# Softmax shares applied by TensorE: a product with a diagonal matrix in place of scaling and turning

## The reference, cut to what matters

```python
p = softmax(where(mask, q @ k.T * scale, -1e30))     # over the branch's keys
o = g[..., 0:1] * (p_c @ v_c) + g[..., 1:2] * (p_s @ v_s) + g[..., 2:3] * (p_w @ v_w)
```

## Time and profile before

| what | value |
|---|---|
| time, median of 3 | 2161.82 us (2155.26 to 2162.44) |
| profiled execution | 2147.99 us |
| its span, first to last instruction | 2146.1 us |
| TensorE busy | 1712.8 us, 80% |
| VectorE busy | 558.3 us, 26% |
| ScalarE busy | 391.6 us, 18% |
| GpSimd busy | 63.7 us, 3% |
| mean granted TensorE clock | 0.928 |

### The profile page before, as it was taken

The page is one execution under the profiler, slowest core; times in us unless marked ns, Lnnn a source line. Parts: engine busy times, 40 slices in busy tenths (PEclk is TensorE's granted clock), DMA queues, the critical chain, the costliest instruction groups (busy, mean ns, idle before and its releaser), DMA issues.

```text
span 2146.1 us, 21293 instructions
## 1 busy us (share of the span) xinstructions
PE 1712.8 (80%) x7510; PEld 803.9 (37%) x7510; DVE 558.3 (26%) x1722; ACT 391.6 (18%) x937; POOL 63.7 (3%) x115
## 2 busy tenths in 40 slices
PE   5998888898888777777369988888978878778772
PEld 2863333344333323332138633434443323223321
DVE  4761334435100000000247603344350000000002
ACT  3111333212111111011031123332121110110110
POOL 0000000000000000000100000000000000000001
PEclk9999999999899999999679999999989989989896
DMA  5421000341799999999343211003427999999993
GB/s 142 97 79 40 26 34 20 113 204 76 312 427 427 429 429 427 429 428 428 146 132 69 79 40 40 20 20 152 172 108 311 428 428 427 429 427 428 429 427 146
DMA packets 119166, 505.73 MB, mean 236 GB/s; under 512 B 37936, under 2 KB 74800, under 8 KB 94512
## 3 DMA queue, kind: packets, MB, share of 16 engines
q1 hardware_dynamic: 107280, 461.75, 53.6%
q0 software_dynamic: 7200, 26.22, 3.2%
q10 hardware_dynamic: 4608, 16.78, 1.9%
HBM read 481.65 MB, written 23.07 MB: 235 GB/s over the span
## 4 chain that ended last, share of the span: by engine, by line
PE 51%; DMA 31%; ACT 5%; DVE 4%; SPq 3%; issue 3%; POOL 1%; POOLq 0%; ACTq 0%; DVEq 0%
DMA arena<-in_expert_up 16%; PE bank L951 14%; DMA arena<-in_expert_gate 12%; PE bank L649 11%; PE bank L670 10%; PE bank L864 5%; SPq L517 3%; PE bank L799 2%; PE bank L831 2%; ACT arena L1128 2%; DMA arena<-in_expert_down 2%; DVE nbias L1550 1%; PE bank L821 1%; PE bank L702 1%; ACT arena L1142 1%
## 5 line engine op out<-in xcount | busy, mean ns | idle before, releaser
L951 PE MATMUL bank<-arena 128*64 128x512 f32 x2688 | 739.6, 637 | 144.5 <-DMA arena<-in_expert_up 86.7
L951 PEld LDWEIGHTS bank<-arena 128*64 128x64 f32 x2688 | 253.8, 146 | 480.8 <-issue 480.8
L670 PE MATMUL bank<-hT,arena 128*128 128x512 f32 x512 | 272.4, 630 | 16.4 <-ACT arena L1107 15.0
L1718 DVE TENSOR_TENSOR arena<-arena,bank 128x512 f32<-128x512 f32 x32 | 22.0, 688 | 909.8 <-PE bank L951 909.8
L951 PE MATMUL bank<-spare_slot,arena 128*64 128x512 f32 x384 | 188.0, 647 | 48.6 <-DMA arena<-in_expert_up 24.7
L1550 DVE TENSOR_REDUCE nbias<-bank 128x1 f32<-128x31 f32 (+4 forms) x192 | 61.6, 383 | 248.8 <-PE bank L802 125.5
L864 PE MATMUL bank<-arena,hT 128*128 128x512 f32 x256 | 113.4, 596 | 4.2 <-DVE hT L1593 4.2
L951 PEld LDWEIGHTS bank<-spare_slot,arena 128*64 128x64 f32 x384 | 55.3, 149 | 163.5 <-issue 163.5
L670 PEld LDWEIGHTS bank<-hT,arena 128*128 128x128 f32 x512 | 85.0, 196 | 79.8 <-issue 50.5
L1128 ACT ACTIVATE arena<-bank,nbias 128x31 f32<-128x31 f32 (+4 forms) x192 | 83.3, 446 | 171.1 <-DVE nbias L1550 139.9
L649 PE MATMUL bank<-arena,hT 128*128 128x256 f32 (+1 forms) x512 | 114.2, 384 | 0.0
(11 more groups left out here) (327 smaller groups left out, 1409.9 us busy)
## 6 DMA issues: line engine op xcount, KB each, us to landing
arena<-in_expert_gate SPq DMA_DIRECT2D x56, 2048.0 KB, 28.1
arena<-in_expert_up SPq DMA_DIRECT2D x56, 2048.0 KB, 30.5
arena<-in_expert_down SPq DMA_DIRECT2D x56, 2048.0 KB, 29.5
arena<-in_w_in SPq DMA_DIRECT2D x26, 1024.0 KB, 5.8
spare_slot<-in_expert_gate SPq DMA_DIRECT2D x8, 2048.0 KB, 26.5
spare_slot<-in_expert_up SPq DMA_DIRECT2D x8, 2048.0 KB, 29.9
y_rows<-arena ACTq DMA_DIRECT2D x32, 512.0 KB, 10.2
spare_slot<-in_expert_down SPq DMA_DIRECT2D x8, 2048.0 KB, 26.9
```

Of the source, the lines that this page charges most:

```text
L670: r = pe.matmul(bank[:, FB, :], lhs, rhs, start=(k == 0), stop=last)
L951: r = pe.matmul(dst[CAP * e:CAP * e + CAP, :], moving[:, k, CAP * e:CAP * e + CAP], slot_of(first + e)[:, k, cols], start=(k == 0), stop=( ...
L1718: TT(hid, silu, bank[:, 3, :], ALU.mult).then_inc(act_ready, 1)
```

## The change

Line 1565's four in-place scalings of `prob` go. In their place VectorE writes one matrix per head, `share`: the identity times the head's shares, in one instruction of 128x512 elements. TensorE then multiplies each block of `prob` (unscaled) by that diagonal matrix, by an ordinary float32 product, where it had turned the scaled block with the identity. The result in PSUM is the same: keys on partitions, each query's column times its share. `share` has two buffers by the parity of n, in a part of the arena that nothing else uses during attention. TensorE waits once for a unit's `share` instead of four times for the scalings.

```diff
+        share = view(126, 2, 4, P)
...
                     c = c0 + kt
                     if c >= 2:
                         pe.wait_ge(evac_act if c % 2 == 0 else evac_dve, c // 2)
+                    if kt == 0:
+                        pe.wait_ge(p_ready, n + 1)
                     for i in range(4):
-                        if kt == 0:
-                            pe.wait_ge(p_ready, 4 * n + i + 1)
-                        r = pe.transpose(bank[0:w, 4 + c % 2, P * i:P * i + P],
-                                         prob[:, n % 2, i, P * kt:P * kt + w], ident[:, :])
+                        r = pe.matmul(bank[0:w, 4 + c % 2, P * i:P * i + P],
+                                         prob[:, n % 2, i, P * kt:P * kt + w], share[:, n % 2, i, :], start=True, stop=True)
                     r.then_inc(tr_done, 1)
...
-                    nk = NCMP if br == CMPB else P * (qt + 1)
                     s = rscale[:, n % 2, :]
...
-                    for i in range(4):
-                        pr = prob[:, n % 2, i, 0:nk]
-                        TS(pr, pr, s[:, i:i + 1], None, ALU.mult).then_inc(p_ready, 1)
+                    TT(share[:, n % 2], mid(ident[:, :], 4), bc(s, P), ALU.mult).then_inc(p_ready, 1)
```

## The result

| | before | after |
|---|---|---|
| time, median (5 runs each) | 2158.34 us (2155.26 to 2162.44) | 2176.11 us (2172.49 to 2181.65) |
| ratio | | 1.0088, 95% interval 1.007 to 1.0106 |
| span of the profiled execution | 2146.1 us | 2170.6 us |
| attention stretch, layer 0 / layer 1 | 196.91 / 196.94 us | 208.02 / 208.01 us |

The change makes the kernel slower by 0.88%. That ratio is not the one of the two medians, which lie 17.8 us or 0.82% apart. The stretches of the last row begin with the first score product and end with the first product of the merge. A second set of runs of the same two kernels gave 1.0126 (1.0095 to 1.0157), medians 2157.19 and 2179.95 us: 22.8 us.

What follows compares the result with a forecast made beforehand. It took attention to be bound by TensorE's turns where no gap hides them: 5.2 + 3.9 + 1.3 + 0 - 0.1 = 10.3 us per layer, 20.5 us for two, giving 2182 us; range 2170 to 2204.

Steps and rivals of the forecast that it cites:

- The second record: On TensorE, a float32 product takes two records where a turn takes one, adding 0.43 us per group of four.
- (a): Attention units in query tiles 0 to 3 where turns set the pace: 12 groups paid in full, 5.2 us per layer.
- (b): Turns of key tiles 2 and 3 in other units, between value products: 9 groups in full, 3.9 us per layer.
- (c): Units with small gaps ahead of the first value product, absorbing part of the added time: 1.3 us per layer remains.
- (d): First two key tiles of other units, 19 groups ahead of gaps of 0.69 us or more: costs nothing.
- the last unit: Attention unit without following scores to hide behind; saved scalings pay for eight more passes, gaining 0.06 us.
- Where it lands: Unit-by-unit placement of 48 groups per layer in attention, costing 10.3 us per layer, 20.5 us for two.
- The clock, 0 in the sum: TensorE clock falls in attention cost 3.3 us per layer; counted as 0, with plus or minus 6.6 in the range.
- no cover: Rival: every added TensorE pass in attention shows, +41 us, 2203 us; chance 0.12 for between forecast and this rival.
- hidden: Rival: copies, not turns, set the attention inner loop's pace; 7.5 us left, 2169 us; chance 0.11.
- faster: Rival: VectorE's queue bounds attention, so saved scalings give 18.6 us back, 2143 us; chance 0.04.
- four times: Rival: on TensorE a product costs four turns' passes, a group growing by 1.3 us, 2244 us; chance 0.03.

Runs made afterwards that it cites:

- run 6: Kernel before, turns of key tiles 0 and 1 issued twice in the 14 units per layer with gaps of 0.69 us or more; ratio to before 1.0008.
- run 2: Kernel before, float32 identity product in place of the turn only for key tiles 0 and 1 (36 of 48 groups per layer); ratio to before 1.0058.
- run 3: Kernel before, float32 identity product in place of the turn only for key tiles 2 and 3 (12 of 48 groups per layer); ratio to before 1.0079.
- run 4: Changed kernel with turns by the identity restored, share written but not read; attention stretches 199.27 / 196.39 us, whole kernel not comparable.
- run 7: Changed kernel with the operation writing share issued twice, TensorE released by the second; ratio to before 1.0098.
- run 11: Kernel before with prob in bf16, scaled in place by VectorE and turned by a bf16 identity product; ratio to before 0.9972.

## Why the prediction was right, by its own steps

- *The second record* was right: 768 records. *Its size* was off: a group grew by 0.50 us ahead of a fill slice and in the loop, and by 0.46 between T1 and P0, not 0.43. A group with 31 stationary columns, for which I took the same, grew by 0.65. In layer 0, between starts at the full clock, (a) and (b) measure 10.3 us where I had 9.1, (c) 1.9 for 1.3, (d) 0.2 for nothing and the last unit 0.1 more than forecast: 12.5 for 10.3. The mistake was to take line 768's two records in 0.22 us, between two other kinds, for a run of eight: in the last unit's sixteen, T0 to P0 took 1.95 us, 0.12 a record.
- *Where it lands* was right but for the fourth unit. The sum was 10.3 us; turns issued twice, which have nearly the forecast's own size (0.44 to a fill slice, 0.43 in the loop), gave 10.9, the later tiles alone 5.8 for 12 groups.
- *(d), nothing:* right, by run 6 and by the gaps. 326.35 had just enough: 2.70 us from T0 to P0 became 2.79.
- *VectorE's saving is idle time:* right. 0.26 became 1.25 us of idle time; alone it brings 0.6 us a stretch.
- *The last unit:* forecast minus 0.06 us, measured plus 0.05.
- *The clock, 0 in the sum:* it gave back 1.7 us a stretch, within the 3.3 that I had allowed. That was luck, and it made my sum look better than it was: 12.8 - 1.7 = 11.1 us against 10.3, 22.2 in both layers against 20.5.
- *The time itself:* I wrote 2182 us on a median before of 2161.8, of three; with five it is 2158.3. So 3.5 of the 6 us between my figure and 2176.1 are the base that I started from, and the rest is the difference between 20.5 and the medians' 17.8.
- *One for one behind attention:* layer 0's expert stage, from its first turns to its last output, took 497.5 us and takes 495.8 (windows 543.65 to 1041.16 before, 556.44 to 1052.25 after), and from the end of attention to that output it is 628.5 us in both.
- The rivals: no cover, hidden, faster, four times each fell, by runs 2 and 6, by run 3, by runs 4, 7 and 11, and by the record counts and their pace. (Rival 4's "other 25 groups" are 27; it changes nothing here.) On the last, the Trainium skill ("TensorE: Matmul & The Clock Gate", Terms) has transpose mode four times faster for FP32; here a group takes 0.97 us against 0.47, twice.

What stays open: why a product's record in a row takes 0.12 us and a turn's 0.11, why a product group with 31 stationary columns starts later after the mask, and what makes the clock fall where it does. The first result's 17.8 us between medians and the 22.8 of the second set bracket the 22.2 us of the stretches.

## What to carry to other kernels

Here a float32 turn through TensorE was one record and the float32 product that replaced it two, so work moved from an engine that waits into that product was paid on the engine that does not. With bf16 operands the product was one record and the shortest of the three, whoever did the scaling. Before moving work off an engine, look at the idle time ahead of its next instruction: if it is there, the saving is worth nothing. Cost such a change unit by unit from the gaps ahead of the first dependent instruction, and take the low-clock time out before comparing two stretches.

## What the hardware showed that I had not expected

- Falls of the granted clock to the 1.2 GHz level inside attention cost, with the one at its beginning, 3.4 to 13.8 us a stretch in kernels that differ little, as much as the change itself. For the kernel before and the changed one the falls inside a stretch came back at the same places in four stretches each; for the one with bf16 products and shares the low-clock time was 4.8 and 6.3 us in one execution and 10.7 and 13.7 in another. Shortening the gaps did not make them fewer: with turns doubled in the gaps the low-clock time rose from 5.1 to 6.8 us.
- Eight float32 product records of 128 columns take 0.97 us to the next instruction, eight records of turns 0.91, four bf16 records 0.22 (0.055 each).
- Products with 31 stationary columns cost more than those with 128: 0.99 us to the fill slice and a start 0.33 us after the mask's product (247.63, 247.96, 248.95 in the changed kernel), against 0.94 and 0.24 at the full width (254.86, 255.10, 256.04); in bf16 0.33 us to the fill slice where the full width takes 0.22. For turns there is no such difference: 0.24 and 0.43 us (247.41, 247.65, 248.08) against 0.23 and 0.44 (254.13, 254.36, 254.80).
